# The running sums of a residual branch's output, added on GpSimd in place of VectorE

## The reference

```
h = rms_norm(x, g_pre) * (1.0 + scale) + shift     # scale, shift, gate from c @ w_ada
y = branch(h)                                      # its last step is a matmul with w_out or w_down
x = x + gate * rms_norm(y, g_post)
```

## Time and profile before

| | |
|---|---|
| median of 3 runs | 3264.58 us (3263.66 to 3268.11) |
| the profiled execution: span from its first to its last instruction | 3265.3 us |
| PE busy | 3117.1 us, 95% |
| DVE busy | 2510.6 us, 77% |
| ACT busy | 1569.2 us, 48% |
| POOL busy | 0.2 us, 4 instructions |
| mean granted TensorE clock | 0.980 |
| HBM | 241 GB/s over the span |

### The profile page before, as it was taken

One profiled execution on the slowest core, in us unless ns is written; L12 is line 12 of the kernel. 1 busy time (PEld: TensorE's weight loads), 2 busy tenths in 40 slices (PEclk: granted clock), 3 DMA queues, 4 the chain that ended last, 5 costly groups with the idle time before them and its releaser, 6 DMA issues. The chain is left out here.

```text
span 3265.3 us, 49414 instructions
## 1 busy us (share of the span) xinstructions
PE 3117.1 (95%) x20322; PEld 2698.4 (83%) x20322; DVE 2510.6 (77%) x3120; ACT 1569.2 (48%) x2327; POOL 0.2 (0%) x4
## 2 busy tenths in 40 slices
PE   4899999999999999999999999999998999999998
PEld 3788878888888878888888888887886888888887
DVE  7997999798888787777887566788569677556665
ACT  2455654344444556765444444445443455333454
POOL 0000000000000000000000000000000000000000
PEclk7999999999999999999999999999999999999999
DMA  9777859888888645553687666775655554554353
GB/s 409 301 306 302 316 228 353 334 334 339 335 337 328 232 180 194 217 209 129 259 327 263 228 229 206 268 259 207 225 173 181 181 182 142 207 181 146 139 184 112
DMA packets 136976, 790.24 MB, mean 242 GB/s; under 512 B 20081, under 2 KB 38897, under 8 KB 46001
## 3 DMA queue, kind: packets, MB, share of 16 engines
q1 hardware_dynamic: 108002, 754.65, 62.1%
q10 hardware_dynamic: 28752, 32.45, 3.0%
HBM read 769.28 MB, written 17.76 MB: 241 GB/s over the span
## 5 line engine op out<-in xcount | busy, mean ns | idle before, releaser
L1518 DVE TENSOR_TENSOR wl<-raw,wh 128x2048 fp32r<-128x2048 f32 x479 | 1096.4, 2289 | 244.1 <-ACT wh L874 243.4
L394 PE MATMUL bk<-HX,wh 128*128 128x512 f32 x4592 | 1113.2, 395 | 2.9 <-ACT wh L874 1.6
L394 PEld LDWEIGHTS bk<-HX,wh 128*128 128x128 f32 x4592 | 842.4, 188 | 176.7 <-ACT wh L874 2.7
L874 ACT ACTIVATE wh<-raw 128x2048 fp32r<-128x2048 f32 x479 | 913.6, 1908 | 33.5 <-DMA raw<-in_w_in 26.4
L394 PEld LDWEIGHTS bk<-HX,wl 128*128 128x128 f32 x4592 | 571.4, 188 | 29.3 <-DVE wl L1518 6.5
L394 PE MATMUL bk<-HX,wl 128*128 128x256 f32 x4592 | 578.8, 278 | 2.6 <-DVE wl L1518 2.6
L394 PE MATMUL bk<-hb,wh 128*128 128x512 f32 x2048 | 494.1, 393 | 5.5 <-ACT hb L874 5.0
L1526 DVE SCALAR_TENSOR_TENSOR raw<-raw,cb 128x2048 f32<-128x2048 f32 x192 | 437.1, 2283 | 13.9 <-DMA raw<-in_w_ada 13.9
L394 PEld LDWEIGHTS bk<-hb,wh 128*128 128x128 f32 x2048 | 376.6, 188 | 82.2 <-ACT hb L874 5.8
L394 PEld LDWEIGHTS bk<-hb,wl 128*128 128x128 f32 x2048 | 256.4, 189 | 12.3 <-DVE wl L1518 1.8
L394 PE MATMUL bk<-hb,wl 128*128 128x256 f32 x2048 | 258.9, 279 | 0.9 <-DVE wl L1518 0.9
(11 more groups left out here) (276 smaller groups left out, 2690.6 us busy)
## 6 DMA issues: line engine op xcount, KB each, us to landing
raw<-in_w_ada SPq DMA_DIRECT2D x192, 1024.0 KB, 6.1
raw<-in_w_up SPq DMA_DIRECT2D x128, 1024.0 KB, 5.2
raw<-in_w_down SPq DMA_DIRECT2D x128, 1024.0 KB, 5.1
raw<-in_w_in SPq DMA_DIRECT2D x68, 1024.0 KB, 5.1
raw<-in_kv_w SPq DMA_DIRECT2D x33, 1024.0 KB, 4.8
raw<-in_w_out SPq DMA_DIRECT2D x32, 1024.0 KB, 4.8
raw<-in_s_w_in SPq DMA_DIRECT2D x32, 1024.0 KB, 4.9
raw<-in_fox_w_in SPq DMA_DIRECT2D x32, 1024.0 KB, 4.7
```

The source lines that it names most:

```text
L394: return e.matmul(o_, l_, r_, start=start, stop=stop, skip_group_check=True)
L874: return e.activation(o_, i_, f, **kw)
L1518: return e.tensor_tensor(o_, a_, b_, op)
```

## The change

`y_add` moves from VectorE's program to a program of its own on GpSimd, which has nothing else in it. The waits, the operands and the count of adds are the same. On VectorE `y_slab` loses its two calls. The add is now issued whenever its three semaphores allow it, and no longer at a fixed place among VectorE's instructions.

```
             def y_slab(i, n):
 
                 if n:
                     y_times_x(i, n - 1)
-                if n >= 3:
-                    y_add(i, n - 2)
                 next_low(TURNS[i] + n)
-                if n == 15:
-                    y_add(i, 14)
...
+        def gpsimd(e):
+
+            def y_add(i, n):
+
+                q = slice(0, 1 if i == 5 else 3)
+                if i == 5:
+                    e.wait_ge(s_yg, 16 * i + n + 1)
+                else:
+                    e.wait_ge(s_y2, 16 * i + n + 1)
+                    e.wait_ge(s_t1, 16 * i + n + 1)
+                if n >= 2:
+                    e.wait_ge(s_yadd, 14 * i + n - 1)
+                e.tensor_tensor(TACC[:, q, :], TACC[:, q, :], TS[n % 3][:, q, :], ALU.add).then_inc(s_yadd, 1)
+
+            for i in range(6):
+                for n in range(1, 15):
+                    y_add(i, n)
```

More of the change, by code:

```diff
@@ L1612, in gate @@
                 return PRM[:, S5_POST:S5_POST + 16]
[L1614 to L1624, removed]
             def y_slab(i, n):
@@ L2431, in _ @@
                 vector(e)
+            @block.gpsimd
+            def _(e):
+                gpsimd(e)
             @block.tensor
```

## The result

The changed kernel takes 3282.21 us (median of 4 runs, 3281.16 to 3282.98), the kernel before 3266.35 us (4 runs). The ratio is 1.0040, with a 95% interval of 1.0027 to 1.0053: **slower by 9 to 17 us**, where 12 were forecast. The profiled span went from 3265.3 to 3281.2 us.

The account below looks back on a forecast made before the run. VectorE was taken to bound turn 0 and partly turn 3, TensorE being full elsewhere. The terms 8.1 + 3.4 + 0.5 summed to +12 us, from 3264.58 to 3276.6 us, with an 8-in-10 range of 3257 to 3285.

Parts of the forecast that it names:

- The bound: Whole kernel: VectorE time matters only where TensorE waits for it, losing 6.3 us in turn 0 and 2.3 in turn 3.
- The hold: Each GpSimd add takes 1.62 us, between 0.95 and 2.29, and VectorE waits out its whole length.
- The period: Turn 0, from one w_ada product to the next on VectorE: 5.27 + 1.62 = 6.89 us against 6.15, or +0.74.
- Turn 0: First of six stretches holding the adds, VectorE nearly full: 11 adds at +0.74 us give +8.1 us.
- Turn 3: Fourth stretch, adds among S5 table work: ten adds at +0.74 us less 4.0 us idle time give +3.4 us.
- The other turns: Turns 1, 2, 4 and 5, TensorE full: VectorE's idle time hides holds of about 0.2 us, so 0.
- The end of a turn: Before TensorE's sums, which need add 14: in turn 0 that add ends late, costing at most +0.5 us.
- The fifth instruction stream: Launch of GpSimd's own program, costed at nothing.
- no interference: Rival: GpSimd reads beside VectorE at no cost, turns 0 and 3 gain, -6.9 us in total, 3257.7 us; chance 0.20.
- the add that slips under "joined": Rival: the add starts only while VectorE's PSUM-reading instruction runs; +3.5 us in turn 0, total 3268.1 us; chance 0.15.
- The longer add: Rival: each add takes 2.29 us and holds VectorE throughout; +27 us, 3291 us; chance 0.08.
- the late last add: Rival: an add ends over 3 us late, all six turns wait at the sums, 1 us each; no separate chance given.

Follow-up runs that it names:

- e8: The changed kernel with one column in every add (sums left out); ratio to the kernel before 0.9972 (0.9962 to 0.9981).
- e1: Adds on GpSimd in turn 0 only, on VectorE elsewhere, against the kernel before; ratio 1.0027 (1.0017 to 1.0037).
- e3: Adds on GpSimd in turns 1, 2, 4 and 5 only, against the kernel before; ratio 1.0006 (0.9998 to 1.0015).
- e4: The changed kernel, but in turn 0 GpSimd's add also waits for VectorE's following low half; ratio to the kernel before 1.0038 (1.0027 to 1.0050).
- e6: The kernel before plus 14 extra 768-column adds of constants on GpSimd in turn 0; one run 3289.72 us (before: 3264.57 to 3274.41).
- e7: The kernel before plus two GpSimd fills of 768 columns per block in turn 0; one run 3262.67 us (before: 3264.57 to 3274.41).
- e9: The kernel before plus a 1024-column GpSimd add of constants per slab in turn 1, after the low half; one run 3274.49 us (before: 3270.23).
- e2: Adds on GpSimd in turn 3 only, on VectorE elsewhere, against the kernel before; ratio 1.0010 (1.0002 to 1.0019).
- e10: The kernel before plus one 768-column, one-operand GpSimd instruction per block in turn 0; one run 3274.09 us (before: 3270.23).

## Why the prediction was right

The prediction's mechanism and its sign held, and the time lies within 6 us of it. That two of its terms came so close to the measured ones, the hold and turn 3, is luck.

- *The bound.* VectorE sets turn 0 and in part turn 3, and nothing else (e8: 5.52 us a slab once it is relieved; e1 to e3).
- *The hold.* Forecast 1.62 us, the middle between 0.95 and 2.29; measured 1.65. The period: forecast 6.89, measured 6.91. VectorE paid 0.88 us for the add and now pays 1.65. The middle of two bounds has no mechanism behind it, so its size was luck: the forecast was an add of 1.62 us that holds for its whole length, and the runs show a row of 1.85 us where GpSimd's add is alone (e4) and a hold of 0.2 us less.
- *The pages.* The Trainium skill, SBUF — State Buffer, section "Who interferes with whom", had the rule; e6, e7 and e9 agree with each clause of it that they tried: two SBUF operands are held (1.27 us), writes don't hold (0), an instruction with one operand in PSUM is free (0.42 us inside the add). The estimate of 1.86 us worked out from the Trainium skill, GPSIMD Engine Reference, section "Elementwise — side-by-side cycle accounting", agrees with GpSimd's own row where it is alone (1.85 us in e4), not with the hold.
- *Turn 0.* Forecast +8.1, measured +10.05. The term was mis-sized by its count: I took eleven adds away and put eleven holds in. The add of a block now starts as soon as its operands are there, ahead of the low half of the same slab, and one slab earlier than in VectorE's order. So twelve holds count up to the last late low half: eleven on low halves, (50.2 - 14 x 2.29) = 18.1 us, and one of 1.5 us on the short `mod` row. 18.1 + 1.5 - 11 x 0.88 = 9.9 us.
- *Turn 3.* Forecast +3.4, from ten adds at +0.74 less 4.0 us of idle time; measured +3.7, and +4.2 in e2. The sum was right and its parts were not. Up to the last slab there are twelve holds: four on aq at 1.66 us, four on yt<-y,yt at 0.63 and four at 1.2, or 14.0 us, against 12 x 0.88 = 10.6 us of adds. VectorE's idle time took up nothing of it: its wait ahead of "joined" went from 3.8 to 5.2 us. Shorter holds and unused idle time cancelled.
- *The other turns.* Forecast 0, with a short hold of 0.2 us in turn 1 that did not come (yt<-y,yt keeps 0.43 us); e3's interval is -0.6 to +5 us, and the stretches between the sums of turns 1 and 2 are 354.0 and 354.3 us before and after. The end of a turn: forecast at most +0.5; in turn 0 the last add starts at 458.27 and TensorE comes to TACC at 460.60, 5.5 us after its last slab began, as before. The fifth instruction stream, costed at nothing, cost nothing: TensorE's slab 2 of turn 0 starts at 367.03 us, 367.13 before.
- *The rest of the 16 us.* The profiled spans differ by 15.9, of which 13.8 are these turns. In the S5 layer's output stage, where GpSimd is idle, the changed kernel lost some 3 us among short matmuls. Between the sums of turns 3 and 4 it took 464.3 us against 461.3; e6, with GpSimd idle there too, took 464.2, and the others 460.2 to 462.7. The stretch before turn 3's sums varied from 746.6 to 756.6 us over the kernels. I take the rest for such variation; it was not tried further.

The rivals: no interference is refuted by e6, the add that slips under "joined" by the changed kernel's own rows (GpSimd gets in at the next instruction boundary, though VectorE had no gap) and, where it was forced in e4, it gave 3.0 us in turn 0 and not the rival's 4.6 (8.1 less 3.5). The longer add and the late last add did not come.

No version here that moves the adds and keeps the computation whole beats the kernel before. In turn 0 the hold is 2.15 ns a column (1.65 us over 768), and VectorE paid 1.15 (0.88 over 768). By that no share of the columns is worth moving there; no run moved a part of them and kept the rest on VectorE. e3 shows nothing to gain in the turns where VectorE has idle time.

## What to carry to other kernels

An add moved from VectorE to GpSimd is not gone from VectorE when its neighbours read two SBUF operands: it comes back as a longer row of an instruction that was not touched. Where VectorE is the bound, compare the hold (here 1.65 us) with what the add took from the period (0.88 us), not with its own row. Where VectorE has idle time the move is harmless as far as e3 can tell, and also worth nothing. By e7 and e9, what can run on GpSimd beside a full VectorE is work that only writes, or as much as fits beside VectorE instructions that read PSUM; no run here moved such work.

## What was not expected of the hardware

- A GpSimd instruction with one operand lasted longer than the add with two: 2.45 us (e10) against 1.79 (e6) for 768 columns (both rows have about 0.4 us of waiting for VectorE's add in them), while its hold on VectorE was shorter, 0.63 against 1.27 us.
- At the same 768 columns an add of constants held VectorE for 1.27 us (e6) and the add of TACC and TS for 1.65: the hold depends on more than the width.
- A row of 16 columns (0.18 us before in the same place) was held to 1.7 us: the hold does not ask how short the other instruction is.
- The loads of turn 0 reached 392 GB/s at 99% of the DMA engines' time in e8, above the 361 GB/s at 97% in the earlier trace rows: the rate at a given share is not a fixed one, and my bound from it was too low.
